# Expert weights of a mixture-of-experts block: each matrix requested by one transfer with runs of 8 KB in place of two with runs of 4 KB

## The reference, cut to what matters

```python
scores = jax.nn.sigmoid((xt @ w_router).astype(jnp.float32))     # 64 experts, top 8 per token
...
def expert_block(args):
    tok, e = args
    xb = xt[tok]
    hb = jax.nn.silu(xb @ w1[e]) * (xb @ w3[e])     # w1[e], w3[e]: 1024 x 256
    return hb @ w2[e]                               # w2[e]: 256 x 1024
yb = lax.map(expert_block, (row_tok.reshape(n_blocks, EXPERT_BLOCK), blk_e))
routed = jnp.zeros_like(xt).at[row_tok].add((yb.reshape(P, D) * row_w[:, None]).astype(xt.dtype))
```

## Time and profile before

| what | value |
|---|---|
| time before, median of 3 runs | 2138.23 us (2137.22 to 2140.28) |
| the profiled execution's own time | 2136.88 us |
| its span, first to last instruction | 2135.0 us |
| PE busy | 1907.8 us, 89% of the span |
| DVE, ACT, POOL busy | 1316.2, 1014.5, 461.7 us |
| q1 (SP's transfers) | 292.82 MB, 38.2% of 16 engines |
| q0 (POOL's transfers) | 103.16 MB, 19.9% of 16 engines |
| mean granted clock of TensorE | 0.949 |

### The profile page before, as it was taken

How to read it: one execution, slowest core, us unless ns; L and a number is a source line. 1 busy time by engine, 2 the same in 40 slices (tenths; PEclk the granted TensorE clock), 3 DMA queues, 4 the chain that set the end, 5 groups by cost and what they waited for, 6 DMA issues and landing times. The chain is left out here.

```text
span 2135.0 us, 31401 instructions
## 1 busy us (share of the span) xinstructions
PE 1907.8 (89%) x8693; PEld 1366.6 (64%) x8694; DVE 1316.2 (62%) x2397; ACT 1014.5 (48%) x1850; POOL 461.7 (22%) x338
## 2 busy tenths in 40 slices
PE   3999998775899988999799999999999999999992
PEld 3788886453788854444366667667766666666661
DVE  6566713874688734434365676666666666666664
ACT  3322213664444422222255666666656666656663
POOL 0000000201222101223322333333332233232330
PEclk9899999996999988999889999999999999999996
DMA  9065204003110046311278979899979998899965
GB/s 352 36 208 216 88 3 114 14 16 127 41 46 6 10 148 265 90 50 61 87 229 260 318 224 300 242 302 347 284 217 324 335 306 263 238 321 293 314 165 177
DMA packets 129923, 396.86 MB, mean 186 GB/s; under 512 B 22724, under 2 KB 35101, under 8 KB 126766
## 3 DMA queue, kind: packets, MB, share of 16 engines
q1 hardware_dynamic: 97134, 292.82, 38.2%
q0 software_dynamic: 32720, 103.16, 19.9%
HBM read 337.72 MB, written 77.94 MB: 195 GB/s over the span
## 5 line engine op out<-in xcount | busy, mean ns | idle before, releaser
L2086 DVE TENSOR_TENSOR w_low<-w_experts,w_high 128x1024 fp32r<-128x1024 f32 x392 | 454.5, 1221 | 141.1 <-ACT w_high L2046 114.2
L2046 ACT CAST w_high<-w_experts 128x1024 fp32r x392 | 382.0, 1046 | 49.8 <-issue 49.3
L2160 PE MATMUL ps_y<-w_experts,actT 128*128 x768 | 349.7, 598 | 19.8 <-issue 15.2
L2137 PE MATMUL ps_h<-w_high,xT_high 128*128 128x512 f32 x776 | 317.3, 409 | 9.0 <-DVE xT_low L2092 8.8
L2137 PE MATMUL ps_h<-w_low,xT_high 128*128 128x512 f32 x776 | 309.2, 399 | 0.0
L2137 PE MATMUL ps_h<-w_high,xT_low 128*128 128x512 f32 x776 | 308.7, 398 | 0.0
L2027 POOL DMA_INDIRECT acc<-y_rows,scatter_idx x96 | 154.2, 1606 | 684.0 <-DVE idx L2079 360.1
L2160 PEld LDWEIGHTS ps_y<-w_experts,actT 128*128 128x128 f32 x768 | 139.2, 191 | 162.9 <-issue 162.8
L2070 ACT COPY y_rows<-ps_y 128x512 f32<-128x512 f32 x96 | 56.5, 588 | 259.8 <-PE ps_y L2160 254.8
L2137 PEld LDWEIGHTS ps_h<-w_high,xT_high 128*128 128x128 f32 x776 | 147.9, 191 | 42.5 <-issue 6.7
L2137 PEld LDWEIGHTS ps_h<-w_high,xT_low 128*128 128x128 f32 x776 | 147.1, 190 | 35.8
(11 more groups left out here) (429 smaller groups left out, 3170.7 us busy)
## 6 DMA issues: line engine op xcount, KB each, us to landing
w_experts<-in_exp_w SPq DMA_DIRECT2D x384, 512.0 KB
qT<-in_w_ada POOLq DMA_DIRECT2D x16, 1024.0 KB, 5.2
w_raw<-in_w_in SPq DMA_DIRECT2D x24, 512.0 KB, 7.4
w_ada<-in_w_ada SPq DMA_DIRECT2D x8, 1024.0 KB, 11.9
pb<-pb_tile SPq DMA_DIRECT2D x16, 256.0 KB, 2.7
w_out<-in_w_out SPq DMA_DIRECT2D x1, 4096.0 KB, 16.7
x_kept<-x SPq DMA_DIRECT2D x8, 512.0 KB
acc_tile<-acc SPq DMA_DIRECT2D x8, 512.0 KB, 6.3
```

What stands on the lines that cost most here:

```text
L2046: act.copy(w13_s[par][0][:, which, k], w13[:, bass.ds(w, 1), which, k].squeeze(1)).then_inc(w_high, 1)
L2086: dve.tensor_tensor(w13_s[par][1][:, which, k], w13[:, bass.ds(w, 1), which, k].squeeze(1), w13_s[par][0][:, which, k], ALU.subtract).then ...
L2137: q = pe.matmul(ps_h[:].rearrange("p (a n) -> p a n", a=2), xT[a][:, k, :], w13_s[par][z][:, :, k, :], start=(k == 0 and m == 0), stop=(k ...
L2160: q = pe.matmul(ps_y[n][:], aT[:, k, :], w2[:, bass.ds(w, 1), k, n * BANK:(n + 1) * BANK].squeeze(1), start=(k == 0), stop=(k == FC - 1))
```

## The change

In `load_up` and `load_down` the loop over halves is gone, and one `dma_start` asks for a whole matrix: 1 MB, with 8 KB contiguous on each of the 128 partitions. An expert takes three transfers in place of six. Since fewer transfers add to the semaphores, SP's waits count to half as much. Nothing else is changed: the bytes, the order of the matrices, what SP waits for and when.

```diff
-                    sp.wait_ge(w2_in[before], turn * 32 + (32 if s else 0))
+                    sp.wait_ge(w2_in[before], turn * 16 + (16 if s else 0))
...
-                sp.wait_ge(w13_in[s], turn * 64 + 64)
+                sp.wait_ge(w13_in[s], turn * 32 + 32)
...
-            sp.wait_ge(w2_in[SLOTS - 1], E // SLOTS * 32)
+            sp.wait_ge(w2_in[SLOTS - 1], E // SLOTS * 16)
...
     w13 = keep["w_experts"][:, s, 0:2 * KC * F].rearrange("p (a k f) -> p a k f", a=2, k=KC)
     for which, name in enumerate(("exp_w1", "exp_w3")):
         view = io[name][0].rearrange("e (p k) f -> e p k f", p=P)[bass.ds(e, 1)].squeeze(0)
-        for half in range(2):
-            k = slice(half * KC // 2, (half + 1) * KC // 2)
-            eng.dma_start(w13[:, which, k], view[:, k, :]).then_inc(keep["w13_in"][s], 16)
+        eng.dma_start(w13[:, which], view).then_inc(keep["w13_in"][s], 16)
...
     view = io["exp_w2"][0].rearrange("e (p k) d -> e p k d", p=P)[bass.ds(e, 1)].squeeze(0)
-    for half in range(FC):
-        eng.dma_start(w2[:, half], view[:, half, :]).then_inc(keep["w2_in"][s], 16)
+    eng.dma_start(w2, view).then_inc(keep["w2_in"][s], 16)
```

## The result

The changed kernel takes 2178.72 us (median of 4 runs, 2175.61 to 2185.14) against 2138.52 us: a ratio of 1.0181, 95% interval 1.0148 to 1.0214, about 40 us slower. The time lies inside the predicted range, 2133 to 2182 us, and on the predicted side, but near its upper end: the forecast was +17 us. The span of the profiled execution grew from 2135.0 to 2179.8 us, by 44.8 us.

A forecast was written before the change was run, and what follows sets the result against it. The prediction took PE to bound the expert stage, with the DMA engines close behind. Terms of 18 - 1 = +17 us on the profiled 2136.88 us gave 2153.9, and 2155 us as the median; range 2133 to 2182 us.

The forecast's parts named there:

- PE is the bound, and earlier weights bring next to nothing: Expert stage: PE busy 961 of 982 us, DMA engines close behind; PE waited only 4.6 us for weights.
- An 8 KB run is one unit when the queues take turns, 1.2 us per scatter: Scatter beside a weight load: eight rows per engine each wait 0.313 us, not 0.160, so it lands 1.2 us later.
- Earlier weights, -1 us: PE's 4.6 us of waits for weights: shorter loads save part, -1 us, with ends 0 and -4.6.
- The gather "pays less", costed at nothing: Gathers on q0 behind the scatter: burst nearly spent, issued three blocks ahead; no term in the sum.
- the reads of `tab`: Ahead of `down`: 15.2 us of PE waits without a releaser, put down to slow table reads, at worst 1.65 us.
- The way through DVE, 18 us: DVE's waits for scatter landings delay `xT_low` and PE's `up`; covers counted turn by turn give 18 us.
- PE's busy time, taken as unchanged: Expert stage: PE busy 961 us at full granted clock; only its waits were costed.
- The rival "much slower", 2183 us: Scatter beside a load starts later, lead counted in transfers or packets, landing up to 2 us later; +46 us, chance 0.13.
- The rule of 1 MiB per transfer: Weight loads: the skill page asks at least 1 MiB per transfer for bandwidth; weighed as speaking for the change.
- The fit: Weight loads: 2.0 us plus bytes at 436 GB/s per transfer, making an expert 19 us before, 13 us after.
- The rival of the slow phases clearing faster: Weight burst runs through up to 2.2 us sooner, ahead of the scatter; about -8 us, 2130 us, chance 0.17.

The follow-up runs named there:

- run4_tr1024: Kernel before with one 1 MB transfer per matrix, runs kept at 4 KB by separating the pieces in the slot: 2138.25 us, ratio 0.9995.
- run2_tr512: Kernel before with 512 KB transfers kept, but each 4 KB put in two places of 2 KB: 2116.68 us, ratio 0.9879.
- before_gf: Kernel before (4 KB runs) with every gather issued one block earlier: 2119.56 us, ratio interval 0.9866 to 0.9912.
- up8: Kernel before with the changed form (8 KB runs) for w1 and w3 alone, w2 as before: 2175.45 us, ratio 1.0177.
- after_idx4: Changed kernel with four buffers for the scatter's index in place of two: first run 2192.95 us, ratio interval 1.0218 to 1.0282.
- run8_tr512: Changed kernel's 8 KB runs, but two 512 KB transfers per matrix, for partitions 0 to 63 and 64 to 127: 2428.66 us, ratio 1.1361 to kernel before.
- run8_tr512_alt: Changed kernel's 8 KB runs, but two 512 KB transfers per matrix, for even and odd partitions: 2164.03 us, ratio 1.0105 to kernel before.

## Why the prediction was wrong

*PE is the bound, and earlier weights bring next to nothing*: right. The load took less of the engines' time (q1's share 53.5% to 49.3%), and nothing came of it.

*An 8 KB run is one unit when the queues take turns, 1.2 us per scatter*: right. It measured 1.4 us of engine time over eight rows where both queues are busy; the landing beside a load grew by 0.7 us in the turn shown and by 1.2 us on average, and run4_tr1024, run2_tr512 and the changed kernel order themselves by the run.

*Earlier weights, -1 us*: wrong in sign. PE's waits for weights went from 4.6 to 6.6 us, where the prediction had them stay below 5.

*The gather "pays less", costed at nothing*: this is the step that failed. I argued from its distance of three blocks and from the burst being nearly spent. In the changed kernel PE's waits for rows rose from 0.3 to 12.3 us and the wait ahead of `down` by 2.5 us, together 14.5 us that the sum put at nothing. The trace of before held the warning, 15.2 us ahead of `down`, which I put down to the reads of `tab` alone; issuing the gathers a block earlier takes that wait away and 24 us of time (before_gf).

*The way through DVE, 18 us*: the path is right and in the trace, the price is not a fixed one. On PE the waits for DVE's work went from 0.6 to 12.0 us, on the weight loads, which overlap, from 2.4 to 25.0 us. With the gathers early in both kernels the change costs 36 us, twice the 18, while PE waits 30.3 us for DVE's work against 5.6. Counting covers turn by turn in the trace of before takes the other waits of PE as given, and the table above shows that they are not: the two ways can't be priced apart and added.

*PE's busy time, taken as unchanged*: it grew by 17.1 us in the stage, about 8.5 us of it from the clock that falls behind long waits (the estimate above). The sum has no term for it.

*The rival "much slower", 2183 us*, came nearest in size, for a reason that does not hold: its scatter was to begin later by up to 2 us because the lead is counted in transfers. In the set of scatters named above the first packet comes 4.9 us after the issue before and 5.1 us after the change, 0.2 us later. The rival of the slow phases clearing faster named a gain, and the time went the other way.

*The rule of 1 MiB per transfer*, weighed in the prediction, brought nothing: the Trainium skill, page "DMA: Bandwidth & Descriptors", section "Rules for kernel authors", gives it for bandwidth, and run4_tr1024 shows 2138.25 us with 1 MB transfers against 2137.76 us with 512 KB. The 512 KB transfers moved 421 GB/s already. The fit that the prediction took from the same page stands there for transfers that GpSimd issues, and these are SP's.

What stays open: the interaction of run and transfer size (1.05% against 1.81%), the 14.4 us of waits for w2 in up8, why after_idx4 is slower than the changed kernel, the last 13 us, and the part of PE's 17 us of longer busy time that is not the clock.

## What to carry to other kernels

When a bulk load shares the DMA engines with small transfers that someone waits for, look at the length of the bulk load's runs: here it set how long each small packet stood in line. Shorter runs made the kernel faster (2 KB: 1.2%), longer ones slower, while the DMA engines' own work moved the other way. Before costing a later landing, list every engine that waits for a landing, and look just upstream of a wait without a releaser for a landing that came late; two such ways can replace each other, so cut both before judging either.

## What the hardware did that I had not expected

- A transfer into 64 neighbouring partitions ran at half the rate: 0.58 us per 8 KB packet and 232 GB/s in run8_tr512, against 417 GB/s when each transfer goes to every second partition (run8_tr512_alt).
- A scatter's first packet comes 2.2 us after its issue where q1 is quiet. Beside a load it comes 5.2 us after it, and each engine works off another 57 KB of weights in that time with 4 KB runs and 62 KB with 8 KB runs (means over the scatters with the full lead, a reading of the packets in order of time).
- After 3 us without work the granted clock of TensorE was 0.66 on average over the next 5 us, in the middle of a stage whose mean is 0.99. It fell behind waits of 1.3 us too, as at 1178 us, where PE had waited 1.32 us for rows and 0.70 us ahead of `down`.
